# The last eight row tiles: five summed by VectorE and three by TensorE, against all eight by TensorE

## The chip, the cores and the metric

The kernel runs on one core of one Trainium2 chip. The metric is the device time of one execution in microseconds. Times below are counted from the start of the profiled span unless they are called a run's time.

## The reference

One encoder layer on a sequence of 1,024 tokens with 1,024 features, in float32: a token-mixing part, then a mixture of experts, then a final RMSNorm. Only the end matters here:

```
u2 = modulate(rmsnorm(x, norm_ffn_g[l]), sh_ffn, sc_ffn)
x = x + gt_ffn[:, None, :] * moe_ffn(u2, w_router, router_bias, w_exp_gate[l], w_exp_up[l], w_exp_down[l])
return rmsnorm(x, final_g)
```

Each token has two experts out of 32, with weights w0 and w1 that add to 1. So a token's last row is x + w0 y0 + w1 y1 (y0, y1: its two experts' outputs, already times gt_ffn), divided by the root of its mean square, times final_g.

## The kernel before

The token mixing fills the first part of the run, then the 32 experts follow in a fixed order. An expert's tokens are processed in blocks of 32 (78 of them in all). Every block's outputs go to a table d_y in device memory (line 728, issued by POOL). What follows the last block is the stretch that the change touches. It has eight tiles of 128 tokens each, t = 0 to 7, and all five sequencers have a part in it:

- POOL waits until the last blocks are stored (line 749), and then issues 16 indirect DMAs (line 753): for each tile the gather of y0[t] and the gather of y1[t], 128 rows of 4 KB each (0.52 MB a gather, 8.4 MB in all). Both count on the semaphore ld_y[t], which reaches 32 when both have landed.
- The residual rows x1 (0 to 32 KB of each partition) have been in SBUF since the token mixing.
- VectorE builds the diagonal matrices pair_diag for the tiles of ON_PE = (2, 4, 6) (line 1808): the identity times w0 or w1, one matrix for each of the two. Then it runs a hand-written order of add_pair and final_row: pairs 0, 1; rows 0, 1; pair 3; row 2; pair 5; rows 3, 4; pair 7; rows 5, 6, 7. add_pair(t) waits for ld_y[t] and adds w0 y0 and w1 y1 into x1 (lines 1818 and 1819). final_row(t) waits for the root of tile t, takes its reciprocal (line 1825) and writes res[t] (line 1826).
- TensorE does tiles 2, 4 and 6 (line 1113): for each 512-column half, identity times x1, diagonal 0 times y0 and diagonal 1 times y1 are accumulated in one PSUM bank. A tile has a pair of banks, 2j and 2j+1, used once. mix_ps counts finished tiles.
- ScalarE squares each total with a sum along the row (line 1383, out of x1 or of PSUM), and takes the root (line 1384), tile by tile in order.
- The SP queue waits for fin_ready and stores res[t] (line 582), 0.52 MB a tile, in order; the kernel ends when all have landed.

The gathers travel on the DMA queue q0 (software descriptors, issued by POOL), the stores on q1 (hardware queue, issued by SP). The same 16 DMA engines serve both.

Of the kernel before, what the change touches and what calls it, by code (L numbers as in the profile page):

```python
# [8 lines left out]
P = 128  # L9
TT = T // P  # L10
# [33 lines left out]
QT = D // 4  # L44
EPS = 1e-6
NEG = -1e30
ON_PE = (2, 4, 6)
QUAD = 32


# [59 lines left out]
def build(nc, x, c, ada_w, ada_b, norm_mix_g, norm_ffn_g, w_in, w_branch_gate, b_branch_gate,  # L110
# [6 lines left out]
    ADD, SUB, MUL = ALU.add, ALU.subtract, ALU.mult  # L117

    ctx = ExitStack()
    with ctx:  # L120
# [3 lines left out]
        def at(name, kb, shape, dt=f32):  # L124
            return nc.alloc_sbuf_tensor_at(name, shape, dt, offset=base + int(kb * 1024))

        def sem(name):
            return ctx.enter_context(nc.semaphore(name))
# [57 lines left out]
        x1 = at("x1", 0, [P, TT, D])  # L186
# [32 lines left out]
        y0 = [at(f"y0_{t}", 32 + 4 * t, [P, D]) for t in range(TT)]  # L219
        y1 = [at(f"y1_{t}", 64 + 4 * t, [P, D]) for t in range(TT)]  # L220
# [2 lines left out]
        fing = at("fing", 148, [P, D])  # L223
        res = [at(f"res{t}", 96 + 4 * t, [P, D]) for t in range(TT)]
        junk2 = at("junk2", 128, [P, D])
        pair_diag = at("pair_diag", 132, [P, len(ON_PE), 2, P])


        NM = ["score", "sel", "hit", "wgt", "rank", "slot", "ta", "tb"]
# [22 lines left out]
        def small(name, shape, dt=f32):  # L252
            n = 1
            for s in shape[1:]:
                n *= s
            t = at(name, cur[0], shape, dt)
            cur[0] += (n * 4 + 31) // 32 * 32 / 1024
            assert base + cur[0] * 1024 <= nc.sbuf_usable_end, name
            return t

        ident = small("ident", [P, P])
# [30 lines left out]
        pair_w = small("pair_w", [P, 2, TT])  # L292
# [3 lines left out]
        ps = ctx.enter_context(nc.psum_tensor("ps", [P, 8, HALF], f32))  # L296
# [38 lines left out]
        mo_ps, x1_half, root2, u2_ready, x2t_ps, u2T_ready, ro_ps = (sem(n) for n in (  # L335
            "mo_ps", "x1_half", "root2", "u2_ready", "x2t_ps", "u2T_ready", "ro_ps"))
# [10 lines left out]
        gate_ready, diag_ready, mix_ps, fin_root, fin_ready = (sem(n) for n in (  # L347
            "gate_ready", "diag_ready", "mix_ps", "fin_root", "fin_ready"))
        ld_y = [sem(f"ld_y{t}") for t in range(TT)]
# [30 lines left out]
        HF = [slice(0, HALF), slice(HALF, T)]  # L380
# [377 lines left out]
        def _(pe):  # L758
# [29 lines left out]
            n = 11 * BC + 3 * KC  # L788
# [168 lines left out]
            for b in range(3):  # L957
                with pe.Fori(0, KC // 2) as two:
                    for s in range(2):
                        it = two * 2 + (b * KC + s)  # L960
                        k = it + GATE0
# [4 lines left out]
                        for h in range(2):  # L966
                            pe.wait_ge(gated, 2 * it + (h + GATED_PRIME - 3))
                            n = 0
                            for kc in range(BC):
                                for w, x in ((w_pr_hi, br_hi[b]), (w_pr_hi, br_lo), (w_pr_lo, br_hi[b])):  # L970
                                    n += 1
                                    last = pe.matmul(ps[:, 2 * s + h, :], w[s][:, kc, :], x[:, kc, HF[h]], start=(n == 1), stop=(n == 3 * BC))  # L972
# [10 lines left out]
            for t in range(TT + 3):  # L983
                if t < TT:
                    for h in range(2):
# [5 lines left out]
                        n = 0  # L991
                        for kc in range(KC):
                            if t == 0 and kc % 2 == 0:
                                pe.wait_ge(wo_ready, WO_PIECES * h + kc // 2 + 1)
                            for a, b in ((m_hi, wo_hi), (m_hi, wo_lo), (m_lo, wo_hi)):
                                n += 1
                                last = pe.matmul(ps[:, q % 4, :], a[t % 2][:, kc, :], b[h][:, kc, :], start=(n == 1), stop=(n == MM))  # L997
                        last.then_inc(mo_ps, 1)
                if t >= 3:
# [3 lines left out]
                    for kc in range(KC):  # L1003
                        last = pe.matmul(ps[:, 6, (t - 3) * NE:(t - 2) * NE], u2T[:, kc, :], wr[:, kc, :], start=(kc == 0), stop=(kc == KC - 1))  # L1004
                    last.then_inc(ro_ps, 1)
                if 2 <= t <= TT + 1:
                    pe.wait_ge(u2_ready, t - 1)
                    v = u2[:, t - 2, :].rearrange("p (q c) -> p c q", c=KC)
                    for kc in range(KC):
                        last = pe.transpose(ps[:, 4 + kc // 4, (kc % 4) * P:(kc % 4 + 1) * P], v[:, kc, :], ident[:])  # L1010
# [7 lines left out]
            for t in range(TT):  # L1018
                last = pe.matmul(ps[:, 7, TT * NE:(TT + 1) * NE], ones_b[:], hit_b[:, t, :], start=(t == 0), stop=(t == TT - 1))
# [11 lines left out]
            for i in range(2 * TT):  # L1031
                if i == TT:
                    pe.wait_ge(late_hits, 1)
                for q in range(P // CAP):
                    last = pe.matmul(ps[CAP * q:CAP * (q + 1), 2, 0:LIST], lane_hit[:, i, :], turn_hit[:, i, :],
                                     start=(i == 0), stop=(i == 2 * TT - 1))
# [43 lines left out]
            def down_of_last_block(p):  # L1080
                pe.wait_ge(wd_ready, p)
                pe.wait_ge(actT_ready, p)
                pe.wait_ge(y_evac, p)
                down()
# [20 lines left out]
                    hidden_rows(p)  # L1105
            down_of_last_block(ends[NE - 1])

            pe.wait_ge(diag_ready, 1)
            for j, t in enumerate(ON_PE):
                pe.wait_ge(ld_y[t], 32)  # L1110
                for h in range(2):
                    for i, (a, b) in enumerate(((ident[:], x1[:, t, HF[h]]), (pair_diag[:, j, 0, :], y0[t][:, HF[h]]), (pair_diag[:, j, 1, :], y1[t][:, HF[h]]))):
                        last = pe.matmul(ps[:, 2 * j + h, :], a, b, start=(i == 0), stop=(i == 2))
                last.then_inc(mix_ps, 1)


# [1 line left out]
        def _(sc):  # L1118
            ch = Chain(sc, ch_act)
# [88 lines left out]
            for cc in range(BC):  # L1208
                k = 2 * cc + 2
# [3 lines left out]
                for i, bank in enumerate((4, 7)):  # L1213
                    ins = sc.activation(flat(z[:, 0, 2 * i:2 * i + 2, :]), ps[:, bank, :], ACT.Copy)
# [105 lines left out]
            for i in range(2 * WO_PIECES):  # L1320
                h, q = i // WO_PIECES, i % WO_PIECES
# [51 lines left out]


            for t in range(TT):
                if t in ON_PE:
                    j = ON_PE.index(t)
                    sc.wait_ge(mix_ps, j + 1)
                    total = ps[:, 2 * j:2 * j + 2, :].rearrange("p a n -> p (a n)")
                else:  # L1380
                    sc.wait_ge(x1_half, 2 * TT + t - sum(m < t for m in ON_PE) + 1)
                    total = x1[:, t, :]
                ch(sc.activation(junk2[:], total, ACT.Square, accum_out=ms2[:, t:t + 1]))
                sc.activation(rstd2[:, t:t + 1], ms2[:, t:t + 1], ACT.Sqrt, scale=1.0 / D, bias=eps[:]).then_inc(fin_root, 1)

# [2 lines left out]
        def _(dve):  # L1388
            ch = Chain(dve, ch_dve)
# [62 lines left out]
            for kc in range(KC + 1):  # L1452
# [4 lines left out]
                if kc:  # L1457
                    m = kc - 1
# [118 lines left out]
            for b in range(3):  # L1577
# [5 lines left out]
                with dve.Fori(0, KC // 2) as two:  # L1583
                    blk = two + b * (KC // 2)
                    ch.enter(two, (4, 8, 4)[b])
                    for s in range(2):
                        dc = two * 2 + s
                        it = dc + b * KC
                        if b < 2:
                            for h in range(2):  # L1590

                                kc, p = 4 * s + 2 * h, 2 * s + h
# [26 lines left out]
            for i in range(2 * WO_PIECES):  # L1619
                h, q = i // WO_PIECES, i % WO_PIECES  # L1620
# [10 lines left out]
            for t in range(TT + 2):  # L1631
# [7 lines left out]
                if 1 <= t <= TT:  # L1639
                    m = t - 1  # L1640
# [152 lines left out]
            last = 2  # L1793
            for i in range(NE):
# [7 lines left out]
                last = end  # L1802
            output_of_last_block(last)


            for j, t in enumerate(ON_PE):
                for k in range(2):
                    ins = dve.tensor_scalar(pair_diag[:, j, k, :], ident[:], pair_w[:, k, t:t + 1], None, MUL)
                    if j == len(ON_PE) - 1 and k:
                        ins.then_inc(diag_ready, 1)  # L1810
                    else:
                        ch.mark(ins)
            dve.wait_ge(ld_rows, 16 * 6)

            def add_pair(t):

                dve.wait_ge(ld_y[t], 32)
                ch(dve.scalar_tensor_tensor(x1[:, t, :], y0[t][:], pair_w[:, 0, t:t + 1], x1[:, t, :], MUL, ADD))
                dve.scalar_tensor_tensor(x1[:, t, :], y1[t][:], pair_w[:, 1, t:t + 1], x1[:, t, :], MUL, ADD).then_inc(x1_half, 1)

            def final_row(t):

                total = ps[:, 2 * ON_PE.index(t):2 * ON_PE.index(t) + 2, :].rearrange("p a n -> p (a n)") if t in ON_PE else x1[:, t, :]
                dve.wait_ge(fin_root, t + 1)
                ch(dve.reciprocal(ms2[:, t:t + 1], rstd2[:, t:t + 1]))
                dve.scalar_tensor_tensor(res[t][:], total, ms2[:, t:t + 1], fing[:], MUL, MUL).then_inc(fin_ready, 1)

            add_pair(0)
            add_pair(1)
            final_row(0)  # L1830
            final_row(1)
            add_pair(3)
            final_row(2)
            add_pair(5)
            final_row(3)
            final_row(4)
            add_pair(7)
            for t in range(5, TT):
                final_row(t)


# [48 lines left out]
```

## Time and profile before

| | us |
|---|---|
| three runs | 1670.70, 1673.38, 1681.93 |
| median | 1673.38 |
| profiled execution, its time | 1671.21 |
| profiled execution, its span | 1669.5 |
| span's start to the last product of the experts | about 1622 |
| from there to the end of the span | about 47 |

The profile has one execution, so a stretch read from it is compared with that execution's own time, 1671.21 us. Engines are written PE (TensorE matmul), PEld (TensorE weight load), DVE (VectorE), ACT (ScalarE), POOL (GpSimd) and SPq (the queue issued by SyncE). The granted clock of TensorE is given as a share of full speed: 0.50 is 1.2 GHz and 1.00 is 2.4 GHz.

### The profile page before, as it was taken

The numbers are of one execution on the slowest core, as the hardware profiler recorded it, in microseconds if no ns is written. First come the engines' busy times: TensorE is split into PE (matmuls) and PEld (weight loads), VectorE is DVE, ScalarE is ACT, GpSimd is POOL, SyncE is SP. The second block draws the span as 40 slices with busy tenths as digits, with TensorE's granted clock in tenths as the row PEclk, the third lists the DMA queues.
The fourth block names the chain that finished last, engine by engine and source line by source line (L and its number), as shares of the span: only waits on it lengthen the run. The fifth ranks groups of instructions, "written<-read, shape, count | busy, mean of one in ns | idle before, by whom it ended". The sixth has DMA issues, their size and how long they took to land.

```text
span 1669.5 us, 32476 instructions
## 1 busy us (share of the span) xinstructions
PE 1494.3 (90%) x12731; PEld 1052.0 (63%) x12731; DVE 826.9 (50%) x1192; ACT 433.8 (26%) x804; POOL 533.6 (32%) x458
## 2 busy tenths in 40 slices
PE   3899999999989999999998995698699697979884
PEld 3677786777768877887886884354355354545441
DVE  4555534555653235444226656355265355546455
ACT  4555533444551112002002210111112111111112
POOL 2522233333434242333322110343243233324324
PEclk9899999999999999999999995799799899989997
DMA  9660012222214333351115107699999999997968
GB/s 344 163 215 26 26 54 76 64 73 67 61 36 138 116 100 108 106 164 51 57 69 190 41 38 277 239 355 402 405 381 400 403 402 402 401 403 266 402 245 302
DMA packets 173438, 336.66 MB, mean 202 GB/s; under 512 B 27816, under 2 KB 96096, under 8 KB 173360
## 3 DMA queue, kind: packets, MB, share of 16 engines
q1 hardware_dynamic: 144960, 281.12, 45.6%
q0 software_dynamic: 19680, 37.65, 6.6%
q10 hardware_dynamic: 8720, 16.80, 3.3%
q8 instruction: 56, 0.92, 0.2%
q14 instruction: 22, 0.18, 0.0%
HBM read 307.22 MB, written 28.19 MB: 201 GB/s over the span
## 4 chain that ended last, share of the span: by engine, by line
PE 74%; DMA 15%; DVE 5%; issue 2%; ACT 2%; POOL 1%; SPq 1%; POOLq 0%; DVEq 0%; ACTq 0%
PE ps L806 28%; PE ps L1060 13%; DMA w_exp<-in_w_exp_up 11%; PE ps L972 7%; PE ps L1070 6%; PE ps L997 5%; PE ps L870 2%; PE ps L843 2%; DMA ada<-in_ada_w 2%; PE ps L931 1%; PE ps L896 1%; PE ps L942 1%; PE ps L1044 1%; PE ps L1004 1%; DVE br_lo L1555 1%
## 5 line engine op out<-in xcount | busy, mean ns | idle before, releaser
L1060 PE MATMUL ps<-w_exp,xT 128*32 128x256 f32 x4992 | 303.1, 397 | 61.0 <-DMA w_exp<-in_w_exp_up 59.8
L806 PE MATMUL ps<-u_hi,w_hi 128*128 128x512 f32 x768 | 309.3, 403 | 5.3 <-DVE u_lo L1460 5.2
L806 PE MATMUL ps<-u_lo,w_hi 128*128 128x512 f32 x768 | 300.9, 392 | 0.0
L806 PE MATMUL ps<-u_hi,w_lo 128*128 128x512 f32 x768 | 300.7, 392 | 0.0
L1060 PEld LDWEIGHTS ps<-w_exp,xT 128*32 128x32 f32 x4992 | 160.9, 114 | 172.2 <-issue 80.3
L609 POOL CAST w_hi<-w_raw 128x1024 fp32r<-128x1024 f32 x48 | 62.8, 1307 | 380.6 <-PE ps L806 229.8
L1785 DVE COPY w_down<-w_exp 128x4096 f32<-128x4096 f32 x78 | 179.8, 2306 | 0.0
L806 PEld LDWEIGHTS ps<-u_hi,w_hi 128*128 128x128 f32 x768 | 145.4, 189 | 44.4 <-issue 9.2
L806 PEld LDWEIGHTS ps<-u_hi,w_lo 128*128 128x128 f32 x768 | 145.3, 189 | 31.0
L806 PEld LDWEIGHTS ps<-u_lo,w_hi 128*128 128x128 f32 x768 | 145.5, 189 | 29.5 <-issue 1.0
L1070 PE MATMUL ps<-w_down,actT 128*32 128x256 f32 x2496 | 154.2, 388 | 6.4 <-DVE w_down L1785 6.4
L728 POOL DMA_DIRECT2D d_y<-yb x78 | 101.8, 1305 | 90.5 <-ACT yb L1358 86.1
L1768 DVE TENSOR_TENSOR act<-act,ps 64x256 f32<-64x256 f32 x78 | 33.1, 425 | 184.4 <-ACT act L1350 184.3
L610 POOL TENSOR_TENSOR w_lo<-w_raw,w_hi 128x1024 fp32r<-128x1024 f32 x48 | 120.3, 2506 | 3.9
L1070 PEld LDWEIGHTS ps<-w_down,actT 128*32 128x32 f32 x2496 | 74.1, 111 | 57.7 <-DVE w_down L1785 6.7
L721 POOL DMA_INDIRECT xg<-d_u,tok_cur x80 | 85.1, 1064 | 65.5 <-POOL tok_cur L718 64.0
L1350 ACT ACTIVATE act<-ps 64x256 f32<-64x256 f32 x78 | 29.4, 376 | 293.9 <-PE ps L1060 293.9
L1301 ACT ACTIVATE gate<-ps,param 128x512 f32<-128x512 f32 x48 | 33.0, 690 | 268.9 <-PE ps L806 237.7
L718 POOL COPY tok_cur<-tokl 128x1 int32 (+1 forms) x80 | 14.9, 186 | 252.0 <-ACT xg_s L1346 208.6
L1775 DVE TENSOR_TENSOR y_s<-ps,gate_q 128x256 f32<-128x256 f32 x78 | 33.1, 425 | 95.1 <-PE ps L1070 89.1
L1358 ACT ACTIVATE yb<-y_s 128x256 f32<-128x256 f32 x78 | 32.6, 418 | 168.6 <-DVE y_s L1775 168.6
L972 PE MATMUL ps<-br_hi,w_pr_hi 128*128 128x512 f32 x192 | 74.9, 390 | 0.3 <-DVE br_hi L1556 0.3
(280 smaller groups left out, 2125.1 us busy)
## 6 DMA issues: line engine op xcount, KB each, us to landing
w_exp<-in_w_exp_gate SPq DMA_DIRECT2D x32, 2048.0 KB, 24.4
w_exp<-in_w_exp_up SPq DMA_DIRECT2D x32, 2048.0 KB, 26.6
w_exp<-in_w_exp_down SPq DMA_DIRECT2D x32, 2048.0 KB, 26.7
ada_g<-in_ada_w ACTq DMA_DIRECT2D x32, 512.0 KB, 3.7
w_raw<-in_w_in SPq DMA_DIRECT2D x24, 512.0 KB, 4.1
w_raw<-in_w_branch_gate SPq DMA_DIRECT2D x24, 512.0 KB, 4.0
d_y<-yb POOLq DMA_DIRECT2D x78, 128.0 KB, 7.9
bias<-d_table SPq DMA_DIRECT2D x48, 192.0 KB
```

Of the source, the lines that this page charges most:

```text
L609: ch(pool.tensor_copy(w_hi[par][:], raw[:]))
L610: pool.tensor_tensor(w_lo[par][:], raw[:], w_hi[par][:].bitcast(f32), SUB).then_inc(w_split, 1)
L721: pool.indirect_dma_start(out=xg[h][:], out_offset=None, in_=u2_rows, in_offset=bass.IndirectOffsetOnAxis(ap=tok_cur[:, h:h + 1], axis=0)) ...
L728: pool.dma_start(d_y[row, :].rearrange("t (n m) -> n t m", n=4), yb[h][:]).then_inc(st_y[h], 16)
L806: ins = pe.matmul(ps[:, 5 + h, :], a[par][:, kc, :], b[:, kc, HF[h]], start=(n == 1), stop=(n == MM))
L843: last = pe.matmul(ps[:, 2 * g + h, :], bd[:, (2 * g + d) * BC + cc, :], xc[:, HF[h]], start=True, stop=True)
L870: pe.matmul(ps[:, bank, fr], z[:, odd, t, off:off + P], tab[:, t, fr], start=(t == 0), stop=(t == TT // 2 - 1))
L972: last = pe.matmul(ps[:, 2 * s + h, :], w[s][:, kc, :], x[:, kc, HF[h]], start=(n == 1), stop=(n == 3 * BC))
L997: last = pe.matmul(ps[:, q % 4, :], a[t % 2][:, kc, :], b[h][:, kc, :], start=(n == 1), stop=(n == MM))
L1060: last = pe.matmul(ps[CAP * n:CAP * (n + 1), 2, 0:QT], x, w[n // 2][:, off:off + QT], start=(kc == 0), stop=(kc == KC - 1))
L1070: last = pe.matmul(ps[CAP * n:CAP * (n + 1), 6, 0:QT], a, w_down[:, off:off + QT], start=(fc == 0), stop=(fc == FC - 1))
L1785: dve.tensor_copy(w_down[:], w_exp[r][:]).then_inc(wd_ready, 1)
```

## The change

All eight tiles are summed by TensorE. VectorE builds 16 diagonal matrices in place of 6, and no longer adds pairs; it only takes reciprocals and writes res, tile 0 to tile 7. On TensorE the products of the identity with the residual rows are separated from the products with y: those of tiles 0 to 3 are issued before the first wait on a gather; those of tile t (4 to 7) are issued after the products of tile t-1 and ahead of the wait for ld_y[t]. Eight tiles share four bank pairs, so the residual products of tile t (4 to 7) first wait until VectorE has written res[t-4]. ScalarE waits on mix_ps for all tiles. The gathers, the stores and their order in each queue are the same.

```diff
-ON_PE = (2, 4, 6)
-        pair_diag = at("pair_diag", 132, [P, len(ON_PE), 2, P])
+        pair_diag = at("pair_diag", 132, [P, TT, 2, P])
...
+            def residual(t):
+                if t >= 4:
+                    pe.wait_ge(fin_ready, t - 3)
+                for h in range(2):
+                    pe.matmul(ps[:, 2 * (t % 4) + h, :], ident[:], x1[:, t, HF[h]], start=True, stop=False)
+
             pe.wait_ge(diag_ready, 1)
-            for j, t in enumerate(ON_PE):
+            for t in range(4):
+                residual(t)
+            for t in range(TT):
+                if t >= 4:
+                    residual(t)
                 pe.wait_ge(ld_y[t], 32)
-                for h in range(2):
-                    for i, (a, b) in enumerate(((ident[:], x1[:, t, HF[h]]), (pair_diag[:, j, 0, :], y0[t][:, HF[h]]), (pair_diag[:, j, 1, :], y1[t][:, HF[h]]))):
-                        last = pe.matmul(ps[:, 2 * j + h, :], a, b, start=(i == 0), stop=(i == 2))
+                for k, y in enumerate((y0, y1)):
+                    for h in range(2):
+                        last = pe.matmul(ps[:, 2 * (t % 4) + h, :], pair_diag[:, t, k, :], y[t][:, HF[h]], start=False, stop=(k == 1))
                 last.then_inc(mix_ps, 1)
...
             for t in range(TT):
-                if t in ON_PE:
-                    j = ON_PE.index(t)
-                    sc.wait_ge(mix_ps, j + 1)
-                    total = ps[:, 2 * j:2 * j + 2, :].rearrange("p a n -> p (a n)")
-                else:
-                    sc.wait_ge(x1_half, 2 * TT + t - sum(m < t for m in ON_PE) + 1)
-                    total = x1[:, t, :]
+                sc.wait_ge(mix_ps, t + 1)
+                total = ps[:, 2 * (t % 4):2 * (t % 4) + 2, :].rearrange("p a n -> p (a n)")
...
-            for j, t in enumerate(ON_PE):
+            for t in range(TT):
                 for k in range(2):
-                    ins = dve.tensor_scalar(pair_diag[:, j, k, :], ident[:], pair_w[:, k, t:t + 1], None, MUL)
+                    ins = dve.tensor_scalar(pair_diag[:, t, k, :], ident[:], pair_w[:, k, t:t + 1], None, MUL)
...
-            def add_pair(t):
-
-                dve.wait_ge(ld_y[t], 32)
-                ch(dve.scalar_tensor_tensor(x1[:, t, :], y0[t][:], pair_w[:, 0, t:t + 1], x1[:, t, :], MUL, ADD))
-                dve.scalar_tensor_tensor(x1[:, t, :], y1[t][:], pair_w[:, 1, t:t + 1], x1[:, t, :], MUL, ADD).then_inc(x1_half, 1)
...
-            add_pair(0)
-            add_pair(1)
-            final_row(0)
-            final_row(1)
-            add_pair(3)
-            final_row(2)
-            add_pair(5)
-            final_row(3)
-            final_row(4)
-            add_pair(7)
-            for t in range(5, TT):
+            for t in range(TT):
                 final_row(t)
```

## Rows read from the trace of the kernel before

**Rows 1.** The page: the span, and its chain that ended last, by engine.

```profile
span 1669.5 us, 32476 instructions
PE 74%; DMA 15%; DVE 5%; issue 2%; ACT 2%; POOL 1%; SPq 1%; POOLq 0%; DVEq 0%; ACTq 0%
```

**Rows 2.** The chain in order of time, from 1580: start, duration (us), what.

```profile
1624.36 4.19 DMA d_y<-yb
...
1629.41 1.01 POOL y L753
...
1649.81 9.81 DMA y<-d_y,pair_s
1659.64 1.29 DVE x L1818
...
1665.13 1.28 DVE res L1826
```

**Rows 3.** Timeline: start, duration, engine, instruction, [idle before <- what ended it].

```profile
1622.92 1.26 DVE L1808 TENSOR_SCALAR pair_diag<-ident,pair_w 128x128 f32<-128x128 f32 x6
...
1636.33 1.29 DVE L1818 SCALAR_TENSOR_TENSOR x<-y,pair_w,x 128x1024 f32<-128x1024 f32 x1 [12.15 <-DMA y<-d_y,pair_s]
...
1643.33 23.45 SPq L582 DMA_DIRECT2D out<-res  x8
...
1653.36 1.29 DVE L1818 SCALAR_TENSOR_TENSOR x<-y,pair_w,x 128x1024 f32<-128x1024 f32 x1 [0.77 <-DMA y<-d_y,pair_s]
```

**Rows 4.** DMA issues, us to landing; issued at 1638.7, 1641.7, 1652.6 and 1666.4.

```profile
y<-d_y,pair_s POOLq DMA_INDIRECT x1, 5.9
...
y<-d_y,pair_s POOLq DMA_INDIRECT x1, 7.7
...
out<-res SPq DMA_DIRECT2D x1, 512.0 KB, 7.0
...
out<-res SPq DMA_DIRECT2D x1, 512.0 KB, 2.6
```

**Rows 5.** DMA queues, 1646 to 1651: packets, MB, share of 16 engines.

```profile
q0 software_dynamic: 263, 0.97, 50.9%
q1 hardware_dynamic: 255, 0.96, 47.1%
```

**Rows 6.** DMA queues, 1645 to 1659.6, and the whole rate from 1651 to 1659.6.

```profile
q0 software_dynamic: 1017, 3.68, 65.2%
q1 hardware_dynamic: 543, 2.00, 33.7%
...
DMA packets 971, 3.49 MB, mean 406 GB/s; under 512 B 118, under 2 KB 118, under 8 KB 971
```

**Rows 7.** Timeline of tile 2 from its gathers to res, TensorE's products first.

```profile
1647.72 1.88 PE L1113 MATMUL ps<-y,pair_diag 128*128 128x512 f32 x4
...
1649.63 1.02 ACT L1383 ACTIVATE junk<-ps 128x1024 f32<-128x1024 f32 x1 [6.22 <-PE ps L1113]
...
1651.31 1.28 DVE L1826 SCALAR_TENSOR_TENSOR res<-ps,ms,fing 128x1024 f32<-128x1024 f32 x1
```

**Rows 8.** Weight loads, one a product, as a measure of its pace.

```profile
1644.10 0.34 PEld L1113 LDWEIGHTS ps<-y,pair_diag 128*128 128x128 f32 x1 [0.52 <-issue]
...
1644.95 0.34 PEld L1113 LDWEIGHTS ps<-y,pair_diag 128*128 128x128 f32 x1 [0.52 <-issue]
...
1647.72 0.19 PEld L1113 LDWEIGHTS ps<-y,pair_diag 128*128 128x128 f32 x1 [0.24 <-issue]
...
1648.15 0.19 PEld L1113 LDWEIGHTS ps<-y,pair_diag 128*128 128x128 f32 x1 [0.24 <-issue]
```

**Rows 9.** Windows: stretch, us, PE PEld DVE ACT POOL busy (x), clock, DMA, GB/s.

```profile
1642.30:1646.00 3.70, 3.70 (x5) 1.63 (x6) 3.52 (x4) 1.08 (x3) 2.83 (x3) 0.50 1.01 337
1646.20:1649.40 3.20, 3.20 (x8) 1.14 (x6) 1.25 (x1) 0.00 (x0) 2.59 (x3) 1.00 0.96 373
...
1661.00:1664.00 3.00, 0.34 (x1) 0.00 (x0) 2.93 (x5) 2.56 (x6) 0.00 (x0) 1.00 0.05 22
```

More of the change, by code:

```diff
@@ L1803, in _ @@
             output_of_last_block(last)
-            for j, t in enumerate(ON_PE):
+            for t in range(TT):
                 for k in range(2):
-                    ins = dve.tensor_scalar(pair_diag[:, j, k, :], ident[:], pair_w[:, k, t:t + 1], None, MUL)
-                    if j == len(ON_PE) - 1 and k:
+                    ins = dve.tensor_scalar(pair_diag[:, t, k, :], ident[:], pair_w[:, k, t:t + 1], None, MUL)
+                    if t == TT - 1 and k:
                         ins.then_inc(diag_ready, 1)
@@ L1813, in _ @@
             dve.wait_ge(ld_rows, 16 * 6)
-            def add_pair(t):
-                dve.wait_ge(ld_y[t], 32)
-                ch(dve.scalar_tensor_tensor(x1[:, t, :], y0[t][:], pair_w[:, 0, t:t + 1], x1[:, t, :], MUL, ADD))
-                dve.scalar_tensor_tensor(x1[:, t, :], y1[t][:], pair_w[:, 1, t:t + 1], x1[:, t, :], MUL, ADD).then_inc(x1_half, 1)
             def final_row(t):
-                total = ps[:, 2 * ON_PE.index(t):2 * ON_PE.index(t) + 2, :].rearrange("p a n -> p (a n)") if t in ON_PE else x1[:, t, :]
+                total = ps[:, 2 * (t % 4):2 * (t % 4) + 2, :].rearrange("p a n -> p (a n)")
                 dve.wait_ge(fin_root, t + 1)
```

## The prediction

> **What bounds the kernel now.** Start with the page's chain by engine: TensorE has 74% of it and DMA 15% [rows 1]. That average is not the limit where the change is. The change touches only what follows the last expert block, so I read the chain in order of time there. It shows four links: the last block's outputs are stored by 1624.36 + 4.19 = 1628.6; POOL issues 16 gathers, the first at 1629.41 and the last at 1649.81; the last one is in flight for 9.81 us and lands at 1659.62; then VectorE adds tile 7 and writes rows 5, 6 and 7, the last beginning at 1665.13 [rows 2]. Line 1826 takes 1.28 us, so the last store is issued at 1666.41, and it lands 2.6 us later [rows 4], at 1669.0; the span ends at 1669.5.
>
> So two things set the end: when the last gather lands, and 1666.41 - 1659.62 = 6.8 us of engine work after it. The first is a matter of bandwidth. The DMA engines are full from about 1638 on: in 1646 to 1651 the two queues take 50.9% + 47.1% of the 16 engines [rows 5], and from 1651 to 1659.6 they move 406 GB/s [rows 6]. The DMA engines are idle (0.05 busy) only from 1661 to 1664, while VectorE works on the last rows [rows 9].
>
> The size of the stage bounds everything. From 1622.9, where the diagonals begin [rows 3], to the end are 46.6 us, 2.8% of the span. One per cent of the kernel is 16.7 us, about what a measurement of this kernel can tell from no change; to win that, more than a third of a stage that has to move 12.6 MB (16 gathers and 8 stores of 0.524 MB; 31 us at 406 GB/s) would have to go.
>
> **The change, part by part.**
>
> *More diagonals.* Six take 1.26 us, 0.21 each [rows 3]; ten more cost 2.1 us of VectorE, so they end at 1626.3 in place of 1624.2. They are hidden behind POOL's wait and the first gathers: no tile is complete before 1636.33 [rows 3]. If that cover were gone, the cost would be the 2.1 us. I take 0.
>
> *Residual products of tiles 0 to 3 ahead.* Eight products at the slow pace of 1644.95 - 1644.10 = 0.85 us [rows 8] are 6.8 us: 1626.3 to 1633.1, again before 1636.33. Cost 0; at the fast pace less.
>
> *VectorE loses ten adds.* Five pairs of 2 x 1.29 us go from it. In front of the end only tile 7's pair counts: 1659.64 to 1662.2. What these adds hold back elsewhere is more than that. Rows 3 and 4 are behind add_pair(5) in VectorE's order, and that waits until 1653.36 for its gathers [rows 3], although tile 3's had landed at 1638.7 + 5.9 = 1644.6 and tile 4's at 1641.7 + 7.7 = 1649.4 [rows 4]. In the changed kernel nothing stands between a tile's landing and its row but its own work.
>
> *A tile's own work.* From tile 2 [rows 7]: four products, 1647.72 to 1649.60 (1.88); ScalarE starts at 1649.63; VectorE's row starts at 1651.31 and ends at 1652.59. From the products' end to the store's issue that is 2.99 us. With about 0.3 for the wake-up and the first weight load: 0.3 + 1.9 + 3.0 = 5.2 us from landing to store, against 6.8 us for tile 7 now. **Gain if the last gather lands as before: 1.6 us.** The engines keep up: tiles arrive 3 us apart or more, and need 6 x 0.43 = 2.6 us of TensorE (the fast pace, 1648.15 - 1647.72 [rows 8]), about 1.5 of ScalarE and 1.5 of VectorE. The new wait of the residual products (tile 7 for res[3]) is over early: tile 3's store is issued near 1649.6, and tile 6 has not landed by then. Behind that wait stand only the products of the same tile.
>
> *When stores are issued, and what they take.* This is the part that the diff does not show. New issue times: tile 0 near 1644 (before 1643.33 [rows 3]: its four products run at the slow pace), tile 1 near 1645.7, tile 2 near 1647.2 (before 1652.6 [rows 4]), tile 3 near 1649.6, tile 4 near 1649.4 + 5.2 = 1654.6, tile 5 near 1659.5. Now rows 3 and 4 are issued after row 2, near 1657.4 and 1658.8 (1652.6 plus VectorE's wait and work), and rows 5 to 7 after all gathers. Stores that come earlier meet gathers that are still in flight. With both queues at work, q0 moved 0.97 MB and q1 0.96 MB in 5 us [rows 5]: an equal split, and the gathers run at half speed. That is the price. Until 1659.6 the stores have moved 2.00 MB [rows 6]. In the changed kernel rows 0 to 4 are all stored in front of the last gather, 5 x 0.524 = 2.62 MB, and row 5 in part. (2.62 - 2.00) MB at 406 GB/s [rows 6] is 1.5 us. Row 5 is issued near 1659.5; if it moves bytes at once, it shares the engines for the last 3 us and takes another 1.5 us; if only 2 us after its issue (store 2 took 7.0 us to land under load [rows 4] and 2.6 without), 0. I take 0.9, between these: the last gather lands 2.4 us later, at about 1662.0.
>
> The Trainium skill, "DMA: Bandwidth & Descriptors", section "Queues, rings and completion order", states this as a rule: every DMA engine goes round the queues for which it has work, one packet of each in turn. By that rule earlier stores must take from the gathers, which speaks against this change; the trace agrees with 0.97 against 0.96 MB. Without it the sum would be the gain of 1.6 us alone.
>
> **Sum.** Last gather +2.4, work after it -1.6, last store 2.6 as now: +0.8 us. The profiled execution (1671.21) would become 1672.0. The profiled time and the three runs are 1670.70, 1671.21, 1673.38 and 1681.93; their median is 1672.3, 1.1 below the median of the three runs. Scatter among executions is larger than my effect. I take 1672.3 + 0.8 = 1673.1.
>
> **Rivals.**
>
> *A, forecast: the stores give the gain back.* The last gather lands 1.5 to 3.0 us later, by the two ends above, less 1.6: -0.1 to +1.4 us. Place: DMA engines, 1651 to 1662. Chance 0.60.
>
> *B, the gain stands.* If gathers keep their speed, for instance since row 5 moves nothing before the end and rows 3 and 4 fill the time in which VectorE now holds stores back, the end is 0.1 to 1.6 us earlier, 1669.6 to 1671.1 on the profiled execution, about 1671 on the base. For it: the idle 3 us at 1661 to 1664 [rows 9] are capacity that the change can use. Against it: they come after the gathers, where row 5 and 6 alone could use them. Chance 0.22.
>
> *C, the other side: TensorE stays at its low clock and becomes the pace.* Its granted clock was 0.50 (1.2 GHz) from 1642.3 to 1646, when it had stood idle before, and 1.00 (2.4 GHz) from 1646.2, after those products [rows 9]. In the changed kernel it idles between tiles whenever a landing takes longer than its work. At the slow pace a tile of 0 to 3 needs 4 x 0.85 = 3.4 us and a later one 6 x 0.85 = 5.1. From 1636.3: 13.7 and 20.4 us make 1670.4, plus 3.0 and 2.6 and the 0.5 at the end: 1676.5, 7.0 us slower, 1679.3 on the base. It decides as soon as landings are closer together than 5.1 us. If only the last tiles are at the slow pace it is 4 x 0.43 = 1.7 more. Against it: four cold products of tile 0 are followed by those of tile 1 at once, which is what raised the clock at 1646. Chance 0.12, of which 0.03 for the full price.
>
> The Trainium skill, "TensorE: Matmul & The Clock Gate", section "Loop structure matters more than you think", warns of just this loop, a DMA wait between groups of products that lets the clock fall. By it the kernel would be near 1679; by the rows, in which three tiles with gaps between them kept 1.00, it is the lesser case.
>
> *D, nothing seen.* Some other shift of a few us in the rest of the kernel, which is not touched, or a disturbed execution as the one at 1681.93. Chance 0.06.
>
> **How the numbers follow.** A: 1672.2 to 1673.7. B: 1670.7 to 1672.2. C: 1674 to 1679.3. A alone holds 0.60; with B, the near part of C, and the scatter of the base (its fast three lie from -1.6 to +1.1 of it) the range is 1669 to 1678. Faster by over 1% would need 16.7 us out of 46.6, of which no case gives more than 1.6: 0.01. Slower by over 1% is more than twice C's price: 0.01. Within 1%: 0.98.
>
> **What would show it.** In the changed profile: 16 diagonals in about 3.4 us; products of the residual over before 1636; line 1113's y products of tile 0 at the slow pace and from tile 1 or 2 on at 0.43; stores issued singly from about 1644, with row 3 before 1651 and row 4 near 1654.6; q0 and q1 with about equal MB from 1646 to near 1659; the last gather landing near 1662 with 11 to 12 us in flight; about 5.2 us from there to the last store's issue, near 1667.2. I am wrong if the last gather lands before 1661 (then B), or if TensorE's products, not landings, set the spacing of the rows (then C).

## The result, and the profile after

The changed kernel takes 1680.70 us (median of 20 runs, 1677.96 to 1689.36) against 1675.77 us (20 runs, 1670.55 to 1681.93) of the kernel before. The ratio is 1.0033, 95% interval 1.0018 to 1.0048: slower by a third of a per cent, about 5.5 us. That is within 1% as forecast, but the prediction's 1673.1 us and its range up to 1678 are too low. The profiled execution took 1678.30 us and has a span of 1676.5, 7.0 more than the profiled one before [rows 1].

The start of the stage didn't move: the first gather is issued at 1629.32, where it was 1629.41 [rows 2]. All of the 7.0 us are lost behind it. TensorE's part of the timeline of the changed kernel (start, us, what, idle before and what ended it):

```profile
1626.10 8.65 PE L1111 MATMUL ps<-x,ident 128*128 128x512 f32 x16 [3.77 <-DVE pair_diag L1812]
1635.90 14.00 PE L1122 MATMUL ps<-y,pair_diag 128*128 128x512 f32 x32 [1.16 <-DMA y<-d_y,pair_s]
1649.74 1.88 PE L1111 MATMUL ps<-x,ident 128*128 128x512 f32 x4
1651.46 3.60 PE L1122 MATMUL ps<-y,pair_diag 128*128 128x512 f32 x8
...
1665.19 1.88 PE L1111 MATMUL ps<-x,ident 128*128 128x512 f32 x4
1666.91 3.60 PE L1122 MATMUL ps<-y,pair_diag 128*128 128x512 f32 x8
```

From tile 0's landing on there is no idle time between the groups. The count at the end of each line is the thing to read: x32 for tiles 0 to 3 is eight MATMULs a tile, and the code has four calls a tile. Ahead of the gathers stand x16 for eight calls. **Each float32 call is two MATMULs.** Tiles 4 to 7 have 4 + 8 = 12.

The chain that ended last, in order of time, from the last landing that stands in it (start, us, what; the two tiles left out, 5 and 6, are the same):

```profile
1630.64 5.22 DMA y<-d_y,pair_s
1635.86 0.04 issue
1635.90 14.00 PE ps L1122 x32
1649.90 1.72 PE ps L1111 x4
1651.62 3.43 PE ps L1122 x8
...
1665.35 1.72 PE ps L1111 x4
1667.07 3.45 PE ps L1122 x8
...
1672.21 1.28 DVE res L1824
```

Before, this chain ran through the last gather and VectorE [rows 2]; now it leaves the DMAs with tile 0's second gather, and TensorE is the path for 34.6 us: 14.0 + 4 x (1.72 + 3.43). Windows of the changed kernel (stretch, us, busy PE, PEld, DVE, ACT, POOL with counts, granted clock, DMA share, GB/s) show the clock beside it:

```profile
1635.90:1649.60 13.70, 13.70 (x32) 6.19 (x33) 4.34 (x6) 5.51 (x10) 10.12 (x11) 1.00 0.97 369
1649.60:1670.40 20.80, 20.80 (x49) 8.93 (x47) 5.79 (x8) 5.64 (x12) 0.00 (x0) 1.00 0.65 265
```

TensorE was at 1.00 (2.4 GHz) from tile 0's products on, where before it was at 0.50 until 1646 [rows 9]. So it is slow at full clock.

The start of the stage differs by about 15 us among profiled executions of these kernels, for reasons ahead of it. Below, a stretch is therefore counted from the first gather's issue, G (all columns are G plus us), and worked out from each profile's timeline and DMA issues (start plus us to landing). Each row is one execution; of e2, e4 to e7 and c2 there is no other.

| kernel | last gather issued | last landing | last store issued | end of span |
|---|---|---|---|---|
| before | G + 20.4 | G + 30.2 | G + 37.0 | G + 40.1 |
| changed | G + 18.8 | G + 30.5 | G + 44.2 | G + 47.2 |
| e1, no residual products of tiles 4 to 7 | 18.7 | 30.5 | 37.4 | 40.4 |
| e2, e1 without the products of y1 | 18.8 | 32.0 | 37.1 | 40.2 |
| e3, before, stores held | 20.8 | 27.0 | 35.3 | 39.3 |
| e4, changed, stores held | 18.8 | 25.2 | 44.1 | 47.2 |
| e5, before, residual products ahead | 20.7 | 30.6 | 39.2 | 42.3 |
| e6, the same program again | 20.3 | 30.3 | 38.8 | 41.8 |
| e7, e5 with filler products | 20.2 | 29.9 | 36.7 | 39.8 |
| c1, four tiles and four | 20.0 | 31.8 | 37.4 | 40.5 |
| c2, c1 with a split last wait | 20.8 | 30.0 | 36.3 | 39.3 |
| c3, c2 with stores held | 20.0 | 26.1 | 34.2 | 38.4 |
| c4, c3 with pair 7 earlier | 19.9 | 25.7 | 33.7 | 38.0 |

### The profile page after: what moved, and what is told of

Same layout as the page of the kernel before. It is cut to its first block, busy times and chain, and to the rows that moved or that the text cites. A ratio compares the mean times of both kernels' runs of the same rounds, so it can differ in the third digit from the quotient of the medians.

```text
span 1676.5 us, 32595 instructions
## 1 busy us (share of the span) xinstructions
PE 1518.6 (91%) x12791; PEld 1062.5 (63%) x12791; DVE 816.4 (49%) x1192; ACT 434.0 (26%) x804; POOL 531.5 (32%) x458
## 4 chain that ended last, share of the span: by engine, by line
PE 75%; DMA 15%; DVE 5%; issue 2%; ACT 2%; SPq 1%; POOL 0%; DVEq 0%; ACTq 0%; POOLq 0%
PE ps L805 28%; PE ps L1059 13%; DMA w_exp<-in_w_exp_up 11%; PE ps L971 7%; PE ps L1069 6%; PE ps L996 5%; PE ps L1122 2%; PE ps L869 2%; PE ps L842 2%; DMA ada<-in_ada_w 2%; PE ps L930 1%; PE ps L895 1%; PE ps L941 1%; PE ps L1043 1%; PE ps L1003 1%
## 5 line engine op out<-in xcount | busy, mean ns | idle before, releaser
L805 PEld LDWEIGHTS ps<-u_hi,w_hi 128*128 128x128 f32 x768 | 145.4, 189 | 44.2 <-issue 9.2
L1367 ACT ACTIVATE yb<-y_s 128x256 f32<-128x256 f32 x78 | 32.6, 418 | 167.9 <-DVE y_s L1779 167.9
## 6 DMA issues: line engine op xcount, KB each, us to landing
w_exp<-in_w_exp_gate SPq DMA_DIRECT2D x32, 2048.0 KB, 25.2
```

The lines of the kernel that those rows point to most:

```text
L805: ins = pe.matmul(ps[:, 5 + h, :], a[par][:, kc, :], b[:, kc, HF[h]], start=(n == 1), stop=(n == MM))
```

## The experiments

### Does the number of products set the pace? (e1)

```diff
                 for h in range(2):
-                    pe.matmul(ps[:, 2 * (t % 4) + h, :], ident[:], x1[:, t, HF[h]], start=True, stop=False)
+                    if t < 4:
+                        pe.matmul(ps[:, 2 * (t % 4) + h, :], ident[:], x1[:, t, HF[h]], start=True, stop=False)
```

(and start=True on the first y product of tiles 4 to 7)

> The changed kernel without the identity products of tiles 4 to 7 (their x1 is left out of the sum); all else, waits included, is kept. Theory P (the number of products sets the pace: every product of the program is two MATMUL instructions of 0.43 us, so a tile costs 8 x 0.43 = 3.43 us for y and 4 x 0.43 = 1.72 for x1): TensorE ends 4 x 1.72 = 6.9 us earlier, near 1663.5, unless a landing holds it by up to 2 us; span near 1669.7 to 1671.5, about 1.000 of before. Theory L (landings set the pace and the products are hidden): span stays at 1676.5, ratio 1.003.

Measured: 1675.40 us, ratio to before 1.0006 (0.9986 to 1.0025), the end at G + 40.4 in place of G + 47.2: 6.8 us less, against 6.9 expected from 16 MATMULs of 0.43. TensorE is still without a pause:

```profile
1638.45 27.73 PE L1123 MATMUL ps<-y,pair_diag 128*128 128x512 f32 x64 [1.10 <-DMA y<-d_y,pair_s]
```

64 MATMULs in 27.7 us are 0.43 each. Theory P holds, and L, in which the products hide behind the landings, has fallen. Even eight MATMULs a tile are TensorE's pace here, not the DMAs'.

### Landings alone, and what earlier stores take from them (e2)

```diff
-                for k, y in enumerate((y0, y1)):
+                for k, y in enumerate((y0,)):
```

(on e1)

> As the last one, and the products with y1 are left out too (the gathers of y1 and the wait for them stay), so a tile costs TensorE 4 x 0.43 = 1.72 us, which is what the prediction took. Theory S (stores that come earlier slow the gathers, as the prediction's sum has it): the last gather lands near 1662.0, the last store is issued near 1667.2, span about 1670.3. Rival: stores take nothing that matters from the gathers: last landing at 1659.6 to 1659.9 as in both kernels, last issue near 1665, span about 1668.

A tile now costs TensorE what the prediction had assumed, but for tile 5 (below). The timeline of TensorE has gaps ended by gathers, and the chain's last landing is this (start, us in flight):

```profile
1652.07 13.26 DMA y<-d_y,pair_s
...
1665.47 1.97 PE ps L1123 x4
```

With G at 1633.31 the last gather lands at G + 32.0 (expected 1662.0 - 1629.4 = 32.6), the last store is issued at G + 37.1 (expected 37.8; the rival 35.6) and the span ends at G + 40.2. The queues of e2 from 1648 to 1663 (packets, MB, share of the 16 engines):

```profile
q0 software_dynamic: 974, 3.55, 60.3%
q1 hardware_dynamic: 681, 2.53, 41.1%
```

Between 1648 and 1663 stores moved 2.53 MB beside the gathers. The step of the prediction on earlier stores was right in kind, and nearly in size: the last gather lands 1.8 us later than before, where the sum had 2.4, although POOL issued it 1.6 us sooner. With the cost that the prediction gave to TensorE, the stage is as long as before, the tail's gain given back.

One tile of e2 shows something else. TensorE had stood idle for 2.73 us ahead of tile 5, and its four MATMULs took 3.59 us, where the other tiles' took 1.95 to 1.98:

```profile
1657.20 3.59 PE L1123 MATMUL ps<-y,pair_diag 128*128 128x512 f32 x4 [2.73 <-DMA y<-d_y,pair_s]
```

Its granted clock was 0.50 from 1657.2 to 1659. Nothing that ended last waited for it; in e5 something does.

### Stores held behind the gathers (e3, e4)

```diff
+            for t in range(TT):
+                sp.wait_ge(ld_y[t], 32)
             for t in range(TT):
                 sp.wait_ge(fin_ready, t + 1)
                 sp.dma_start(out_v[:, t, :], res[t][:]).then_inc(st_rows, 16)
```

e3, on the kernel before:

> The kernel before, with SP waiting for all eight tiles' gathers ahead of the first store. Theory S: the 2.00 MB of stores that moved before 1659.6 no longer stand beside the gathers, which end 4.9 us earlier, near 1654.7; the last store is issued near 1661.5, and eight stores at 0.41 MB/us take 10.2 us from 1655, so the span ends near 1666 to 1667, 3 us less than before (0.998). Rival: the gathers go at POOL's pace and latency, the last lands at 1659.6 all the same, and the stores then end near 1671, 1 to 2 us later than before.

The last landing went from G + 30.2 to G + 27.0, not to G + 25.3: right in sign, 1.7 us short. The end is at G + 39.3, 0.8 earlier; by runs 1676.02 us, ratio 1.0005 (0.9988 to 1.0022), which tells nothing of so small a change. The missing part is POOL's issue. These two lines (ns min/median/max of an issue, first and last start) are of e3 and of e4:

```profile
L755 POOL DMA_INDIRECT y<-d_y,pair_s x16: 933/981/1861, 1644.0 to 1664.8; - x16
```

```profile
L754 POOL DMA_INDIRECT y<-d_y,pair_s x16: 933/937/1012, 1631.1 to 1649.9; - x16
```

With VectorE adding pairs (e3) an issue takes up to 1.86 us and the sixteenth begins 20.8 us after the first. Without (e4) the longest is 1.01 and it is 18.8. Issue by issue the two fit: in e3 the issues of 1.29, 1.86 and 1.32 us have over 1.2 us each of VectorE's instructions with two tiles from SBUF (adds, or a row out of x1) beside them, and the five issues before the first add take 0.93 to 1.01. Not every overlap shows: one issue has an add beside it for 0.90 us and takes 0.93. In e4 rows read from PSUM stand beside issues for up to 0.9 us, and these still take 0.94. And in both kernels the last gather is then in flight for only about 6.3 us, where it was 9.8 and 11.7 with stores beside it.

e4, on the changed kernel:

> The changed kernel with the same hold on the stores. Theory P: TensorE goes at its own pace whatever the gathers do, so the y products still run from 1635.9 to about 1670.3, the last store is issued at 1673.5 and the span is 1676.5 as in the changed kernel, although the gathers end about 5 us earlier. Theory L: the span moves with the last landing, by several us.

The last landing came 5.3 us earlier (G + 30.5 to G + 25.2), and the end stayed at G + 47.2 to a tenth. That is the strongest evidence for theory P: in the changed kernel nothing behind tile 0 waits for a gather. It also sizes the contention by itself: stores beside the gathers cost the last one 5.3 us in this kernel.

### One part alone: the residual products ahead (e5, e6, e7)

```diff
             for j, t in enumerate(ON_PE):
-                pe.wait_ge(ld_y[t], 32)
                 for h in range(2):
-                    for i, (a, b) in enumerate(((ident[:], x1[:, t, HF[h]]), (pair_diag[:, j, 0, :], y0[t][:, HF[h]]), (pair_diag[:, j, 1, :], y1[t][:, HF[h]]))):
-                        last = pe.matmul(ps[:, 2 * j + h, :], a, b, start=(i == 0), stop=(i == 2))
+                    pe.matmul(ps[:, 2 * j + h, :], ident[:], x1[:, t, HF[h]], start=True, stop=False)
+            for j, t in enumerate(ON_PE):
+                pe.wait_ge(ld_y[t], 32)
+                for k, y in enumerate((y0, y1)):
+                    for h in range(2):
+                        last = pe.matmul(ps[:, 2 * j + h, :], pair_diag[:, j, k, :], y[t][:, HF[h]], start=False, stop=(k == 1))
                 last.then_inc(mix_ps, 1)
```

> The kernel before with one part of the change alone: the identity products of tiles 2, 4 and 6 ahead of the gathers, the rest as before. From here on a stretch is counted from the first gather's issue G, since the stage starts at another time in each execution: the kernel before ends at G + 40.1. Theory P (product count): a tile on TensorE goes from 12 to 8 MATMULs of 0.43 us, but tile 7's sum on VectorE ends the stage, so the end stays at G + 40.1 within 0.5. Rival (moving the products ahead is what costs, by the clock or a wait): the end moves by over 1 us.

A miss: the end went to G + 42.3, 2.2 us later, though TensorE has a third less to do after each landing. Its timeline for tiles 4 and 6:

```profile
1652.07 3.70 PE L1116 MATMUL ps<-y,pair_diag 128*128 128x512 f32 x8 [1.93 <-DMA y<-d_y,pair_s]
1659.64 6.67 PE L1116 MATMUL ps<-y,pair_diag 128*128 128x512 f32 x8 [3.87 <-DMA y<-d_y,pair_s]
```

Tile 6's eight took 6.67 us, tile 4's 3.70. The windows ahead of it and on it show why:

```profile
1655.80:1659.60 3.80, 0.00 (x0) 0.00 (x0) 3.71 (x4) 2.55 (x5) 0.00 (x0) 0.90 1.03 419
1659.60:1661.50 1.90, 1.86 (x2) 0.84 (x3) 1.57 (x3) 0.30 (x2) 0.00 (x0) 0.50 0.92 375
```

TensorE was idle for 3.9 us, and its clock fell from 1.00 to 0.50 near the end of that. Tile 6 became the last total that ScalarE waited for, and row 7 came behind it. I tested this with the same program again (e6) and with spare products that fill the gap (e7):

```diff
                 last.then_inc(mix_ps, 1)
+                for h in range(2 if j < 2 else 0):
+                    pe.matmul(ps[:, 6 + h, :], ident[:], x1[:, t, HF[h]], start=True, stop=True)
```

> The same program as e5 once more, beside e7. In e5 TensorE stood idle for 3.9 us ahead of tile 6's products; the granted clock then was 0.50, the products took 6.67 us in place of 3.7, and the end came at G + 42.3. Theory K (the clock: with the identity products gone from between the tiles, TensorE idles long enough for the clock to fall): the same gap, a clock of 0.50 and an end near G + 42 again, though it may fall at another tile. If e5 was a chance delay, the end is at G + 40.1.

> As e5, with two spare identity products (four MATMULs, 1.72 us) into the unused banks 6 and 7 behind the y products of tiles 2 and 4; their result is never read. Theory K: TensorE's gaps are as short as in the kernel before, tile 6's products run at 1.00 in 3.7 us, and the end is at G + 40.1. If the clock isn't the cause, the end stays near G + 42.

e6 ended at G + 41.8, e7 at G + 39.8. Tile 6 in e6, and in e7 with the spare products ahead of it:

```profile
1657.29 6.54 PE L1116 MATMUL ps<-y,pair_diag 128*128 128x512 f32 x8 [4.23 <-DMA y<-d_y,pair_s]
```

```profile
1654.66 1.88 PE L1119 MATMUL ps<-x,ident 128*128 128x512 f32 x4
1658.43 3.70 PE L1116 MATMUL ps<-y,pair_diag 128*128 128x512 f32 x8 [1.89 <-DMA y<-d_y,pair_s]
```

Four more MATMULs in that gap (eight in the program) made it end 2.0 us sooner, of which 0.4 us is an earlier last landing (G + 29.9 against 30.3). Theory K holds: in the kernel before, the identity products between the tiles cost nothing and kept TensorE's idle time short, 1.04 us ahead of tile 6. Taken ahead of the gathers, they are missed there. They are not the whole gap: they are 1.7 us of the 3.9, and tile 6's second gather also landed later, at G + 28.1 in e5 and G + 27.8 in e6 against G + 26.5 before and G + 27.1 in e7. Why it did was not taken apart. In the changed kernel none of this shows, since its twelve MATMULs a tile leave no gap.

### Towards a better split (c1 to c4)

```diff
-ON_PE = (2, 4, 6)
+ON_PE = (0, 2, 4, 6)
...
-            add_pair(0)
             add_pair(1)
             final_row(0)
             final_row(1)
             add_pair(3)
             final_row(2)
+            final_row(3)
             add_pair(5)
-            final_row(3)
             final_row(4)
+            final_row(5)
             add_pair(7)
-            for t in range(5, TT):
-                final_row(t)
+            final_row(6)
+            final_row(7)
```

(on e5)

> Tiles 0, 2, 4, 6 by TensorE with their identity products ahead (each bank pair once), 1, 3, 5, 7 by VectorE, and VectorE's order has row 5 ahead of pair 7 and row 6 behind it. Theory P: TensorE needs 8 x 0.43 = 3.4 us for every second tile and paces nothing. Tile 7 goes from landing through 2.57 + 1.5 + 1.5 = 5.7 us against 6.8 before, and the last gather lands about 1 later because of earlier stores: end near G + 40.0 (before G + 40.1, the changed kernel G + 47.2). If adding a fourth tile to TensorE were what costs, the end would be at G + 42 or later.

1674.46 us, ratio 0.9988 (0.9965 to 1.0010), end at G + 40.5, half a microsecond over the expectation, with the last landing at G + 31.8. A fourth tile on TensorE, when TensorE has every second tile, costs at most 0.4 us here (the kernel before ends at G + 40.1). So "more tiles on TensorE" is not what costs by itself. The clock fell here too:

```profile
1660.73 5.36 PE L1116 MATMUL ps<-y,pair_diag 128*128 128x512 f32 x8 [5.21 <-DMA y<-d_y,pair_s]
```

Tile 6's products were late again, but VectorE takes row 6 behind pair 7 in this order, and pair 7 was added at 1668.2, after row 6's root was ready at 1667.6. So it cost nothing.

c2 gives y0's gather of tile 7 a semaphore of its own, so that VectorE adds it while y1 is in flight:

```diff
-                                            in_offset=bass.IndirectOffsetOnAxis(ap=pair_s[:, k, t:t + 1], axis=0)).then_inc(ld_y[t], 16)
+                                            in_offset=bass.IndirectOffsetOnAxis(ap=pair_s[:, k, t:t + 1], axis=0)).then_inc(ld_y[t] if t < TT - 1 or k else ld_first7, 16)
...
+                if t == TT - 1:
+                    dve.wait_ge(ld_first7, 16)
+                else:
+                    dve.wait_ge(ld_y[t], 32)
                 ch(dve.scalar_tensor_tensor(x1[:, t, :], y0[t][:], pair_w[:, 0, t:t + 1], x1[:, t, :], MUL, ADD))
+                if t == TT - 1:
+                    dve.wait_ge(ld_y[t], 16)
```

> As c1, and VectorE adds w0 y0 of tile 7 when that gather has landed and waits for y1 alone. From the last landing it is 1.28 + 1.5 + 1.5 = 4.4 us: end near G + 38.9.

The end is at G + 39.3 (expected G + 38.9), in one execution. c3 adds the hold of e3 (with 16 for tile 7's count), and c4 also puts pair 7 ahead of row 5:

```diff
             final_row(4)
-            final_row(5)
             add_pair(7)
+            final_row(5)
             final_row(6)
```

> As c2, with all stores held until the gathers have landed. Held stores moved the last landing from G + 30.5 to G + 25.2 beside TensorE's sums alone and to G + 27.1 with VectorE's adds beside POOL's issues. I expect G + 26.5, tile 7's store issued by G + 31, and the eight stores then take 8 x 1.28 = 10.2 us: end near G + 37.5, 2.6 us less than before, a ratio of about 0.9985. Rival: the sum of both directions sets the end, and holding stores leaves it at G + 39 or more.

> As c3, with pair 7 ahead of row 5 in VectorE's order, since both its gathers have landed by then. c3 ended at G + 38.4, with tile 7's pair begun 2.4 us after its last landing. I expect the last store's issue 1.5 to 1.8 us earlier, at G + 32.5, and then the stores themselves as the bound: eight from G + 26.3 at 1.28 each, end at G + 37.0, 3 us less than before (0.998). If VectorE was not what held c3's end, it stays at G + 38.4.

c3 ended at G + 38.4 (1673.83 us, ratio 0.9980, 0.9954 to 1.0005), c4 at G + 38.0 (1671.93 us, ratio 0.9981, 0.9960 to 1.0002). Both expectations were too good by 1 us. In c4 the stores are now what remains; from the last landing to the end, 1664.9 to 1677.2, the line of its packets is:

```profile
DMA packets 1152, 4.19 MB, mean 341 GB/s; under 512 B 128, under 2 KB 128, under 8 KB 1152
```

4.19 MB at the 400 to 410 GB/s that its windows show is 10.3 us, but 12.1 us lie between the first store's issue (G + 25.8) and the end. The other 1.8 us, before the first bytes move and behind the last ones, were left out of my 10.2. Stage for stage c4 is 2.1 us shorter than before. Its interval just includes 1, so by runs it is not shown to be faster than the kernel before. It lies wholly under the changed kernel's interval, which was measured at another time against the same kernel before.

## Why the prediction was wrong

**Failed: the number of products in a tile's own work.** The prediction reads "four products, 1647.72 to 1649.60 (1.88)" [rows 7] and "6 x 0.43 = 2.6 us of TensorE" a tile. The row with x4 is half a tile. The same stretch of the kernel before reads in full, with the two rows ahead of it that the prediction didn't add:

```profile
1642.26 2.05 PE L1113 MATMUL ps<-x,ident 128*128 128x512 f32 x2 [19.82 <-DMA y<-d_y,pair_s]
1644.10 2.93 PE L1113 MATMUL ps<-y,pair_diag 128*128 128x512 f32 x4
1646.86 1.02 PE L1113 MATMUL ps<-x,ident 128*128 128x512 f32 x2
```

That is the first half of tile 2 (x2 and x4) and the start of its second half (x2, then the x4 of rows 7). Grouped by form, line 1113 of the kernel before has these counts over three tiles:

```profile
L1113 PE MATMUL ps<-y,pair_diag 128*128 128x512 f32 x24 | 12.3, 640 | 0.0
L1113 PE MATMUL ps<-x,ident 128*128 128x512 f32 x12 | 7.4, 699 | 20.9 <-DMA y<-d_y,pair_s 20.9
```

24 + 12 over three tiles is 12 a tile, where the loop has 6 calls. The prediction's own windows say it too: 5 and 8 MATMULs in two stretches inside tile 2 [rows 9]. With 12 x 0.43 = 5.15 us a tile against landings 3.4 us apart on average (tile 0's at G + 6.5, tile 7's at G + 30.5), TensorE had to become the bound. That "tiles arrive 3 us apart or more" was off as well: before, tile 3 landed 2.5 us behind tile 2 (G + 15.2, G + 12.7) and tile 6 as much behind tile 5.

In the terms of the prediction's sum: "work after it -1.6" is the term that failed. From the last landing to the last store's issue it was 13.7 us (G + 30.5 to G + 44.2) against 6.8 before, so +6.9. "Last gather +2.4" was +0.3, and the last store took 2.6 as forecast. Even with no tile queued before it, tile 7 has eight y MATMULs behind its landing, not four: 0.3 + 3.4 + 3.0 = 6.7 us, so only 0.1 of the gain of 1.6 was ever there.

Worked out anew from tile 0's first y product as measured (1635.9; the prediction had 1636.3) and the right count: 1635.9 + 4 x 8 x 0.43 + 4 x 12 x 0.43 = 1670.3, plus 3.0 to the store, 2.6 to land and 0.5: 1676.4. Measured 1676.5. The pace of one product, 0.43 us, the 3.0 us behind the products and the 2.6 us of the store were all right; the count was off by a factor of two.

**Right for the wrong reason: rival C.** It forecast TensorE as the pace with 5.1 us for each of tiles 4 to 7 and an end at 1676.5, which is the measured span. But it had six products at the low clock; the trace has twelve at the high one. That the two come to the same time is luck. It got a chance of 0.12, since I asked whether the clock would fall and never whether the count was right. The Trainium skill, "TensorE: Matmul & The Clock Gate", section "Loop structure matters more than you think", warns of loops that wait for a DMA between products. This did not bear on the changed kernel, whose clock was 1.00 from tile 0's products on. The traces of e2, e5, e6, c1 and c2 agree with it: there the granted clock had fallen to 0.50 by the end of idle times of 2.7 to 5.2 us. The prediction set against it that "three tiles with gaps between them kept 1.00"; the rows of the kernel before hold only one such gap, of 1.04 us.

**Right: the contention.** The equal split of two queues at work held: from 1651.3 to 1659.3 of e2, q0 moved 1.70 MB and q1 1.67. e4 against the changed kernel gives 5.3 us for all stores that stand beside the gathers, and e2, which has the product cost that I had assumed, ended 0.1 us from before where the sum said 0.8. But in the changed kernel this decides nothing. Its last gather lands at 1659.8 and its tile 7 is not begun until 1665.

**Right: what is hidden.** Sixteen diagonals took 3.24 us (3.4 worked out) and cost nothing. The products of tiles 0 to 3 ahead are 16 MATMULs, 8.65 us, and not 8 in 6.8 us; they ended at 1634.8, only 1.1 us before tile 0 landed. About the first four ran at 0.86 us, the rest at 0.43. Had the clock stayed low they would, by my estimate of 16 x 0.855, have taken 13.7 us and held tile 0 for 3.9 us. My cover was real, and thinner than I had written.

**Missed as well: the pause that VectorE's adds put on POOL.** With ten adds gone, the last gather is issued at G + 18.8 in place of 20.4. In the changed kernel nobody waits for it, so the gain is lost.

**Not settled.** The runs differ by 5.5 us and the profiled stages by 7.1; the interval reaches to 1.0048, 8 us, so both fit. Why the stage begins at different times from one execution to the next was not looked into.

## What to carry to other kernels

Count a tile's instructions in the trace before pricing a loop that is moved to an engine: the count of a grouped line divided by the trips of the loop, and not the number of calls in the source, and a merged timeline row may hold only a part of one trip. Before giving an engine all tiles of a stream, compare its time per tile with the time between arrivals; here 5.15 us against 3.4. Work that moves ahead of a wait to be "free" can have been what kept TensorE's clock up between waits.

## What the runs showed of the hardware that I had not expected

- A float32 matmul call of 128 x 512 is two MATMUL instructions in the trace, 0.43 us each at the granted clock 1.00 and 0.85 at 0.50: 0.86 us a call.
- Between tiles TensorE's granted clock was 0.50 after an idle time of 2.7 us (e2), 3.7 us (c2), 3.9 us (e5), 4.2 us (e6) and 5.2 us (c1), and still 1.00 after one of 1.9 us (e5, e7). Spare products of 1.72 us in the gap made e7 end 2.0 us ahead of e6.
- Beside VectorE's additions of two SBUF operands single issues of POOL's indirect DMAs take up to 1.86 us in place of 0.94, and the sixteenth begins 20.8 us after the first in place of 18.8 (e3, e4). The Trainium skill, "SBUF — State Buffer", section "Who interferes with whom", has VectorE instructions with two SBUF inputs contend with GpSimd instructions that read SBUF; the traces of e3 and e4 agree as far as they go: they show the delay, but not the port.
- Stores on one queue beside gathers on another: the last gather landed 5.3 us later than with the stores held (the changed kernel against e4), though the gathers move the same bytes in both.
